# The opening of a transformer-stack kernel: order of the first transfers, and both token blocks worked on per k tile

## The reference

```python
f1 = swiglu(rms_norm(x, ffn1_pre_g), ffn1_w_gate, ffn1_w_up, ffn1_w_down)
# swiglu(x, g, u, d) = (silu(x @ g) * (x @ u)) @ d ; widths 1024 -> 2816 -> 1024
x = x + 0.5 * rms_norm(f1, ffn1_post_g)
# then a token mixer and two more FFNs; the mixer of block 2 (moba_attention)
# adds rel_bias_table_2[bucket(distance)] to its logits, with 32 buckets and 8 heads
```

## Time and profile before

| | us |
|---|---|
| median of 3 runs | 992.6 (992.57 to 992.99) |
| profiled execution: device time | 992.94 |
| profiled execution: span, first to last instruction | 991.1 |
| TensorE busy | 985.8 (99%) |
| VectorE busy | 711.4 (72%) |
| ScalarE busy | 486.5 (49%) |

### The profile page before, as it was taken

How to read it: one execution, slowest core, us unless ns; L and a number is a source line. 1 busy time by engine, 2 the same in 40 slices (tenths; PEclk the granted TensorE clock), 3 DMA queues, 4 the chain that set the end, 5 groups by cost and what they waited for, 6 DMA issues and landing times.

```text
span 991.1 us, 14543 instructions
## 1 busy us (share of the span) xinstructions
PE 985.8 (99%) x5302; PEld 835.6 (84%) x5302; DVE 711.4 (72%) x849; ACT 486.5 (49%) x621; POOL 213.2 (22%) x215
## 2 busy tenths in 40 slices
PE   8999999999999999999999999999999999999998
PEld 6888888888888888888888888888888888888887
DVE  5766767775788767676777998677876767666664
ACT  6534343664665533434545444465555445334342
POOL 3313232014100222222112600060000012223230
PEclk9999999999999999999999999999999999999999
DMA  9665656745325555565745625544536356555561
GB/s 311 227 211 171 208 173 199 268 128 192 127 87 170 203 179 204 176 203 178 240 156 177 204 95 196 190 145 148 170 118 222 129 187 233 170 179 201 179 206 44
DMA packets 121065, 178.53 MB, mean 180 GB/s; under 512 B 5808, under 2 KB 82160, under 8 KB 120896
## 3 DMA queue, kind: packets, MB, share of 16 engines
q1 hardware_dynamic: 120048, 174.86, 52.8%
q0 software_dynamic: 576, 1.39, 0.5%
q10 hardware_dynamic: 400, 1.73, 0.5%
HBM read 176.88 MB, written 2.64 MB: 181 GB/s over the span
## 4 chain that ended last, share of the span: by engine, by line
PE 99%; DMA 0%; ACT 0%; SPq 0%; DVE 0%; issue 0%
PE acc L662 11%; PE acc L666 10%; PE acc L665 10%; PE tp L861 10%; PE gu L861 10%; PE gu L866 5%; PE tp L866 5%; PE tp L662 4%; PE tp L666 4%; PE tp L665 4%; PE gu L662 3%; PE gu L666 3%; PE gu L665 3%; PE acc L1141 2%; PE acc L1144 1%; PE acc L1170 1%
## 5 line engine op out<-in xcount | busy, mean ns | idle before, releaser
L2001 DVE TENSOR_TENSOR wlo<-raw,whi 128x2048 fp32r<-128x2048 f32 x140 | 325.5, 2330 | 153.8 <-ACT whi L1361 152.2
L1361 ACT ACTIVATE whi<-raw 128x2048 fp32r<-128x2048 f32 x150 | 285.8, 1908 | 70.2 <-PE acc L666 22.9
L861 PE MATMUL tp<-act_in,whi 128*128 128x512 f32 x432 | 102.9, 390 | 0.0
L861 PE MATMUL gu<-act_in,whi 128*128 128x512 f32 x432 | 102.6, 390 | 0.0
L1898 POOL TENSOR_TENSOR tmp<-tmp 128x256 f32<-128x256 f32 x54 | 39.8, 737 | 276.2 <-DVE tmp L2122 276.2
L1900 POOL TENSOR_TENSOR sil<-sil,tmp 128x256 f32<-128x256 f32 x54 | 88.7, 1642 | 33.7 <-ACT sil L1432 33.7
L861 PEld LDWEIGHTS gu<-act_in,whi 128*128 128x128 f32 x432 | 80.9, 188 | 16.6
L662 PE MATMUL acc<-whi,hT_hi 128*128 128x512 f32 x240 | 94.0, 392 | 0.0
L665 PE MATMUL acc<-wlo,hT_hi 128*128 128x512 f32 x240 | 93.7, 390 | 0.0
L666 PE MATMUL acc<-whi,hT_lo 128*128 128x512 f32 x240 | 93.4, 389 | 0.0
L861 PEld LDWEIGHTS tp<-act_in,whi 128*128 128x128 f32 x432 | 79.8, 188 | 15.7
(11 more groups left out here) (379 smaller groups left out, 1845.0 us busy)
## 6 DMA issues: line engine op xcount, KB each, us to landing
raw<-in_w_in SPq DMA_DIRECT2D x96, 512.0 KB, 4.5
raw<-in_down SPq DMA_DIRECT2D x66, 512.0 KB, 4.1
raw<-in_gate SPq DMA_DIRECT2D x64, 512.0 KB, 4.3
raw<-in_up SPq DMA_DIRECT2D x64, 512.0 KB, 4.7
raw<-in_w_out SPq DMA_DIRECT2D x16, 512.0 KB, 4.7
raw<-in_w_branch_hg SPq DMA_DIRECT2D x8, 512.0 KB, 4.3
raw<-in_w_branch_attn SPq DMA_DIRECT2D x8, 512.0 KB, 4.7
post<-in_post_gains SPq DMA_DIRECT2D x3, 512.0 KB, 6.0
```

Source lines behind the costliest of these rows:

```text
L861: pe.matmul(banks[:, a, :], w_hi[:, i, a * P:(a + 1) * P], both, start=i == 0, stop=False)
L1361: act.activation(split_weights(k)[0], raw[:, k % RING, :], ACT.Copy).then_inc(hi_ready, 1)
L2001: dve.tensor_tensor(w_lo, raw[:, k % RING, :], w_hi.bitcast(F32), ALU.subtract).then_inc(lo_ready, 1)
```

## The change

- Head of `fixed` moves from ScalarE's queue to be SP's first transfer; x and piece 0 come in single k tiles (gate, up: 128 KB each) or quarters (x: 128 KB) in a new order. ScalarE issues up's k tiles 0 and 1 in its place. `hot` and `rel` become one array and one DMA.
- TensorE transposes k tiles 0 and 1 of each block as they come, multiplies each k tile of piece 0 for both token blocks before the next tile, and transposes tiles 2 and 3 of both blocks between the products of tiles 0 and 1. The warm-up between the transposes is 2 and 1 matmuls.
- The bias product moves behind the products of tiles 0 and 1, to another bank.
- ScalarE and VectorE follow that order; piece 1 is split by one k tile instead of two; `x_sums(0, 0)` comes after `fills(T_FFN1, 3)` instead of before piece 1's second part.

Cut to its core, with 8 columns of indent left out (the rest renames the input arrays):

```diff
...
 x_in = [sem(f"x_in{i}") for i in range(2 * TT)]
-part_in = [sem(f"part_in{i}") for i in range(4)]
+x_first = [sem(f"x_first{t}") for t in range(TT)]
+part_in = [sem(f"part_in{i}") for i in range(6)]
 tile_turned, tile_hi, tile_lo = sem("tile_turned"), sem("tile_hi"), sem("tile_lo")
 part_hi, part_lo, warm_ready, fixed_in = sem("part_hi"), sem("part_lo"), sem("warm_ready"), sem("fixed_in")
 head_in, bias_parts_in, tail_in = sem("head_in"), sem("bias_parts_in"), sem("tail_in")
...
 def first_bank(i, a):
-    return tp[:, a // 2, a % 2 * P:(a % 2 + 1) * P] if i else acc[:, a // 2, a % 2, 0:P]
+    banks = (tp[:, 0, :], acc[:, 1, 0, :], acc[:, 0, 1, :], tp[:, 1, :]) if i else \
+        (acc[:, 0, 0, :], acc[:, 0, 1, :], acc[:, 1, 1, :], acc[:, 0, 0, :])
+    return banks[a][:, 0:P]
 def first_place(i, a):
...
         for w, m in enumerate((wg_d[0], wu_d[0])):
             sp.dma_start(dst[:, 2 * a:2 * a + 2, w * FC:(w + 1) * FC],
                          m.rearrange("(k p) n -> p k n", p=P)[:, 4 * j + 2 * a:4 * j + 2 * a + 2, 0:FC])\
-              .then_inc(part_in[2 * j + a], 16)
+              .then_inc(part_in[4 + a], 16)
+    def x_quarter(t, q):
+        sp.dma_start(x[:, t, q * FC:(q + 1) * FC], x_d[t * P:(t + 1) * P, q * FC:(q + 1) * FC])\
+          .then_inc(x_in[2 * t] if q else x_first[t], 16)
+    def first_gate(a):
+        sp.dma_start(raw[:, 0, a * BLK:a * BLK + FC], wg_d[0][a * P:(a + 1) * P, 0:FC]).then_inc(part_in[a], 16)
+    def first_up(a):
+        sp.dma_start(raw[:, 0, a * BLK + FC:(a + 1) * BLK], wu_d[0][a * P:(a + 1) * P, 0:FC])\
+          .then_inc(part_in[a], 16)
     def first_pieces():
-        x_part(0, 0)
-        half_piece(0, 0)
-        x_part(1, 0)
-        half_piece(0, 1)
+        sp.dma_start(fixed[:, 0:G_END + P], fixed_d[:, 0:G_END + P]).then_inc(head_in, 16)
+        x_quarter(0, 0)
+        first_gate(0)
+        x_quarter(1, 0)
+        first_gate(1)
+        x_quarter(0, 1)
+        x_quarter(1, 1)
+        for a in (2, 3):
+            first_gate(a)
+            first_up(a)
         x_part(0, 1)
         half_piece(1, 0)
         x_part(1, 1)
...
         def turn(i):
             t, h = FILLS[u][i]
             pe.wait_ge(x_in[2 * t + h], 16)
-            if i >= 2:
-                fill(u, i, from_x)
-                return
-            for a in range(4):
-                mm = pe.transpose(first_bank(i, a), from_x(t, 4 * h + a), idn)
-                if a < 3 and (i == 0 or a == 1):
-                    mm.then_inc(tile_turned, 1)
-            mm.then_inc(turn_full, 1)
+            fill(u, i, from_x)
+        def turn_tile(i, a):
+            mm = pe.transpose(first_bank(i, a), from_x(FILLS[u][i][0], a), idn)
+            mm.then_inc(turn_full if a == 3 else tile_turned, 1)
         def product(j, t, a, rests=None):
             w_hi, w_lo = (w.rearrange("p (k n) -> p k n", k=4)[:, a, :] for w in split_weights(j))
...
         pe.wait_ge(warm_ready, 1)
         warm_up(7)
         pe.wait_ge(head_in, 16)
-        turn(0)
-        warm_up(3)
-        pe.wait_ge(bias_parts_in, 16 * 2)
-        pe.matmul(gu[0:8, 1, 0:S], rel[:, :], hot[:, :], start=True, stop=True).then_inc(row_product, 1)
-        for a in range(2):
-            pe.wait_ge(tile_lo, 1 + a)
-            pe.wait_ge(part_hi, 1 + a)
-            product(0, 0, a, rests=(part_lo, 1 + a))
-            if a == 0:
-                turn(1)
-        pe.wait_ge(row_copied, 1)
-        for a in range(2):
-            pe.wait_ge(tile_lo, 4 + a)
-            product(0, 1, a)
-        turn(2)
-        filled(u, 1)
+        for i in range(2):
+            pe.wait_ge(x_first[i], 16)
+            turn_tile(i, 0)
+            turn_tile(i, 1)
+            warm_up(2 - i)
+        pe.wait_ge(tile_lo, 1)
+        pe.wait_ge(part_hi, 1)
+        product(0, 0, 0, rests=(part_lo, 1))
+        pe.wait_ge(tile_lo, 2)
+        product(0, 1, 0)
+        pe.wait_ge(x_in[0], 16)
+        turn_tile(0, 2)
+        pe.wait_ge(x_in[2], 16)
+        pe.wait_ge(tile_lo, 3)
+        turn_tile(1, 2)
+        turn_tile(0, 3)
+        turn_tile(1, 3)
+        pe.wait_ge(part_hi, 2)
+        product(0, 0, 1, rests=(part_lo, 2))
+        pe.wait_ge(tile_lo, 4)
+        product(0, 1, 1)
+        pe.wait_ge(bias_parts_in, 16)
+        pe.matmul(acc[0:8, 1, 0, 0:S], rel, hot, start=True, stop=True).then_inc(row_product, 1)
+        pe.wait_ge(tile_lo, 5)
         pe.wait_ge(part_hi, 3)
         product(0, 0, 2, rests=(part_lo, 3))
+        turn(2)
+        pe.wait_ge(tile_lo, 6)
+        product(0, 1, 2)
+        filled(u, 1)
         pe.wait_ge(hi_ready, 1)
         product(0, 0, 3, rests=(lo_ready, 1))
         filled(u, 2)
-        product(0, 1, 2)
+        pe.wait_ge(row_copied, 1)
         turn(3)
         product(0, 1, 3).then_inc(piece_used, 1)
         filled(u, 3)
-        pe.wait_ge(part_hi, 4)
-        product(1, 0, 0, rests=(part_lo, 4))
-        product(1, 0, 1)
+        for a in range(3):
+            pe.wait_ge(part_hi, 4 + a)
+            product(1, 0, a, rests=(part_lo, 4 + a))
         pe.wait_ge(hi_ready, 2)
-        product(1, 0, 2, rests=(lo_ready, 2))
-        product(1, 0, 3).then_inc(gu_first, 1)
+        product(1, 0, 3, rests=(lo_ready, 2)).then_inc(gu_first, 1)
         filled(u, 4)
         for a in range(4):
             mm = product(1, 1, a)
...
         if m:
             act.wait_ge(x_half, bank_n(m - 1, t, 1))
         else:
+            act.wait_ge(x_first[t], 16)
             act.wait_ge(x_in[2 * t], 16)
             act.wait_ge(x_in[2 * t + 1], 16)
         if m or t:
...
     def first_hi(j, a, n):
         cut = slice(a * BLK, (a + n) * BLK)
-        act.wait_ge(part_in[2 * j + a // 2], 32)
+        act.wait_ge(part_in[4 + a // 2 if j else a], 32)
         act.activation(split_weights(j)[0][:, cut], raw[:, j, cut], ACT.Copy)\
            .then_inc(hi_ready if a + n == 4 else part_hi, 1)
-    def first_turned(i, *tiles):
-        for a in tiles:
-            if a == 3 or i and a == 2:
-                act.wait_ge(turn_full, i + 1)
-            else:
-                act.wait_ge(tile_turned, 4 if i else a + 1)
-            ins = act.activation(first_place(i, a)[0], first_bank(i, a), ACT.Copy, scale=first_gain(i, a))
-            if a == 3:
-                ins.then_inc(act_hi_ready, 1)
-            elif i == 0 or a == 1:
-                ins.then_inc(tile_hi, 1)
+    def first_turned(i, a):
+        if a == 3:
+            act.wait_ge(turn_full, i + 1)
+        else:
+            act.wait_ge(tile_turned, (5 if a == 2 else 2 * i + a) + (i if a == 2 else 1))
+        ins = act.activation(first_place(i, a)[0], first_bank(i, a), ACT.Copy, scale=first_gain(i, a))
+        ins.then_inc(act_hi_ready if a == 3 else tile_hi, 1)
     def row_from_bank():
         act.wait_ge(row_product, 1)
-        act.activation(proj[0:8, 0, 0:S], gu[0:8, 1, 0:S], ACT.Copy).then_inc(row_copied, 1)
+        act.activation(proj[0:8, 0, 0:S], acc[0:8, 1, 0, 0:S], ACT.Copy).then_inc(row_copied, 1)
     def first_setup():
...
         act.wait_ge(tail_in, 16 * 3)
         act.activation(fgw_split[:, :, 0, :], fgw[:, :, :], ACT.Copy).then_inc(act_setup, 1)
-    act.dma_start(fixed[:, 0:G_END + P], fixed_d[:, 0:G_END + P]).then_inc(head_in, 16)
-    for dst, src in ((hot[:, :], hot_d), (rel[:, :], rel_d)):
-        act.dma_start(dst, src).then_inc(bias_parts_in, 16)
+    for a in range(2):
+        act.dma_start(raw[:, 0, a * BLK + FC:(a + 1) * BLK], wu_d[0][a * P:(a + 1) * P, 0:FC]).then_inc(part_in[a], 16)
+    act.dma_start(bias_parts[:, :], bias_parts_d).then_inc(bias_parts_in, 16)
     act.wait_ge(pool_step, 1)
     load_table(0, ACT.Silu)
-    first_turned(0, 0, 1, 2)
+    first_turned(0, 0)
     first_hi(0, 0, 1)
-    first_turned(0, 3)
+    first_turned(1, 0)
+    first_turned(0, 1)
     first_hi(0, 1, 1)
+    first_turned(1, 1)
+    first_hi(0, 2, 1)
+    for a in (2, 3):
+        first_turned(0, a)
+        first_turned(1, a)
+    first_hi(0, 3, 1)
     row_from_bank()
-    first_turned(1, 0, 1, 2, 3)
-    first_hi(0, 2, 1)
-    first_hi(0, 3, 1)
-    first_hi(1, 0, 2)
+    first_hi(1, 0, 1)
+    first_hi(1, 1, 1)
     fills(T_FFN1, 2)
+    first_hi(1, 2, 1)
+    first_hi(1, 3, 1)
+    fills(T_FFN1, 3)
     x_sums(0, 0)
-    first_hi(1, 2, 2)
-    fills(T_FFN1, 3)
     hi(2)
     ffn(0, N_FFN1, N_WIN)
     act.wait_ge(row_out, 16)
...
         link(pool.memset(a[1][0:2, :, :], one))
     link(pool.memset(mhalf[:, :], -0.5))
-    pool.wait_ge(part_in[3], 32)
+    pool.wait_ge(part_in[5], 32)
     with nc.allow_non_contiguous_dma(reason="eight columns"):
         pool.dma_start(fgw[:, :, :], win_d.rearrange("(k p) n -> p k n", p=P)[:, :, FOX_GATE:FOX_GATE + 8])\
             .then_inc(tail_in, 16)
...
         if a + n == 4:
             dve.wait_ge(hi_ready, j + 1)
         else:
-            dve.wait_ge(part_hi, a + 1 if j == 0 else 4)
+            dve.wait_ge(part_hi, 3 * j + a + 1)
         w_hi, w_lo = split_weights(j)
```

(45 more changed lines are left out.)

## The result

| | median us | lowest to highest | runs |
|---|---|---|---|
| before | 992.69 | 992.28 to 993.22 | 22 |
| after | 994.23 | 993.50 to 994.99 | 22 |

The account below looks back on a forecast made before the run. TensorE bounds the kernel, busy 985.8 of 991.1 us, so only its 5.3 idle us can give time. First product -0.53, bias product +0.44, waits -0.66 sum to -0.75; likeliest gain 0.7, median 991.9 us, range 991.2 to 992.9.

Parts of the forecast that it names:

- Moved and free: Opening's transfers: smaller ones issue piece 2 at 8.9 instead of 7.1 us, but it still lands near 15.9, at no cost.
- the sum: Opening up to piece 2 on TensorE: -0.53 + 0.44 - 0.66 = -0.75 us, start at 19.82 instead of 20.57.
- Rival B: SP's queue in the opening: issues slow to 0.71 us, piece 2 lands 1.2 late, no gain, 992.6 us; 14%.
- chain behind piece 2: ScalarE reaches piece 2 at 16.2 us, VectorE's split of piece 3 ends at 25.8, TensorE wants it at 26.02.
- Rival C: TensorE before the first product: clock falls to 1.2 GHz for 3.2 us, +1.6 - 0.7, 993.5 us; 6%.
- First product: TensorE's first product of piece 0: starts at 6.70 instead of 7.23 us, 0.53 earlier (0.2 to 0.8).
- Rival D: Opening's transfers: each takes 4.3 us or more whatever its size, first product at 7.0, gain 0.4, 992.2; inside likeliest case's range.
- Bias product: TensorE, now between products instead of in the wait before the first: two passes 0.22 apart, 0.44 us later.
- Waits: TensorE between the opening's products: 0.3 us of waiting left instead of 0.96, so 0.66 earlier.
- The ceiling of 1.1: Later pieces: slacks at piece 3's split (1.20 less 0.2) and before `down` (1.16) limit any gain to some 1.1 us.

## Why the prediction was wrong

**Which step failed.** It is the sentence under "Moved and free": the bytes ahead of piece 2 are the same, so it lands near 15.9 still. It landed at 17.85. The bytes are the same, but not when they are handed over. At 6.4 us, eleven SP issues were out in both kernels: before 11 x 256 KB and ScalarE's 142, together 2,958 KB; after 109 + 10 x 128 and ScalarE's 289, together 1,678. SP's issues stand about 0.47 us apart whatever their size, so 128 KB each hand over at most some 280 GB/s where the stream could carry 377. The stream thinned out between 7.2 and 9.8, and piece 2 came 1.87 later. The runs bear this out from four sides: halved transfers alone cost 1.7 us, a late issue behind 256 KB transfers cost nothing, and fewer SP issues, by a second engine or by two 256 KB transfers, brought the rate back to 331 and 303 GB/s. But the full queue alone doesn't save the forecast. The order of work with the old transfers is still 1.1 us slower than before at the median, where the sum had a gain of 0.75. The second step that failed is the sum itself, whose terms follow below.

The prediction used as proof of a queue that is always full, while that fullness came from the 256 KB. It had the number in hand: 0.48 a transfer was its own term.

**Rival B** had the place and the price, and 14%: a late stream takes the gain from a delay of 1.2 on. The delay was 1.87. Its mechanism was off: it asked for issues that slow to 0.71, while they stayed near 0.47 but for one of 0.95, and a late issue behind a full queue moved piece 2 by 0.5 only and the time not at all. The prediction's chain behind piece 2 held: piece 2 on ScalarE 1.67 later than forecast (17.87 for 16.2) and the split of piece 3 at 25.8 + 1.67 = 27.47; measured 27.44.

**Rival C**, 6%, is seen in kernels near the changed one and not shown in it. Products at the lower level stand in three profiles: with up's tiles on ScalarE, where it came after 2.04 us without work, and with the early bias product and without the warm-ups, where the upper level had not been reached before. Removing three warm-ups from the kernel before makes some of its runs up to 2.4 us slower. But the changed kernel's own profile has the upper level, its 22 times form no two groups, and more warm-ups moved its median by 0.1 only. The rival can't be dismissed, and no run prices it there.

**The terms of the sum.** These are read from the two profiles and carry their scatter of some 0.3. First product: forecast 0.53 earlier, measured 0.32. Gate's tile 0 landed at about 6.1 instead of 5.7, so `whi` started at 6.13, and the same 0.77 as before leads to 6.90; x of block 1 (4.3 us to landing, issued at 2.13) held TensorE's list to the same moment. Rival D, a landing of 4.3 us or more whatever the size, had this part right. Bias product: forecast 0.44, measured 0.62 in the changed kernel and 0.63 put alone into the old one; the change between its small form and the products costs more than two passes 0.22 apart. Waits: forecast 0.3, and some 1.2 were left against 0.96 before; the one of 0.33 at 15.11 hangs on up of piece 1 landing late. So instead of 0.75 earlier piece 2 starts 0.32 earlier, 0.62 later and 0.27 later, together the 0.57 later that the timeline shows.

**What held.** The order for both blocks per k tile runs as simulated in the one profile in which its feeders were in time and the bias product early: piece 2 at 20.08, with waits of some 0.3. The ceiling of 1.1 wasn't put to the test: no version started piece 2 more than 0.49 earlier. The Trainium skill, DMA: Bandwidth & Descriptors, section Rules for kernel authors, had warned to coalesce; but it puts the overhead below 64 KB, and here 128 KB was too small, for the sake of the issue and not of the transfer. The same page, section Issuing engines are not separate DMA queues, calls the sequencer time that a second issuing engine saves usually small relative to the transfer. For one transfer the trace agrees, 0.43 us of issue against 4.3 to landing; but in the opening SP's issues follow one another, and two of them moved to ScalarE raised the stream from 222 to 331 GB/s.

**Still open.** Some 0.15 us of the loss lie outside the span: device time less span is 1.79 before and 1.94 after in the median, near 1.8 in every kernel with the old order of work and 1.85 to 2.02 in those with the new. No run here tells why; every kernel with the new order also has `hot` and `rel` merged into one array, and the two were not tried apart. The rest of the 1.54 us needs no further cause: 1.1 are the difference of the profiled spans, and 0.3 are there because the profiled execution before is slower than its median by 0.25 and the one after faster by 0.05. Nor is it shown how stream and order share the loss in an average execution, nor why the new order stays 0.6 above before with old transfers, early bias product and warm-ups.

## What to carry to other kernels

A DMA queue is fed in bytes per issue: divide the size of a transfer by the time from one issue to the next (here 128 KB by 0.47 us, some 280 GB/s) and compare it with what the stream carries (here 377); where the quotient is the smaller, splitting the transfers delays what lies behind them, however early the first piece lands. Two causes that delay different paths to the same wait do not add up, so removing one of them gives back less than it costs alone. Before work is thinned out ahead of the first matmuls, look at what keeps TensorE at its upper clock, and run often enough to see two groups of times. Where TensorE waits early, look first for an order of its own list that closes the wait, before touching the transfers: one moved line gave a likely 0.35 us here, where the whole reordering lost 1.5.

## What the runs showed of the hardware

- TensorE's rise to the upper level came at different times in executions of nearly the same opening: with the same seven warm-ups from 1.20 on, by 5.1 us in the kernel before, by about 6.6 and 7.5 in the ones with the late issue and with one line moved, and only at about 9.9 and 10.3 us in the profiled executions without the later warm-ups and with the early bias product.
- The granted clock in the windows read 1.00 over a stretch at the lower level in two kernels (early bias product, no warm-ups) while 512 columns stood 0.43 apart, and 0.59 in another (up's tiles on ScalarE). The Trainium skill, TensorE: Matmul & The Clock Gate, section Seeing it yourself, calls the recorded clock events unreliable; the trace agrees.
- Five transfers of 4 bytes a partition took 2.39 us to issue, 0.48 each; issues of 128 or 256 KB stood 0.47 apart.
- The bias product (8 rows by 256, two passes 0.22 us apart), put between large products, delayed the next instruction by 0.62 and 0.63 us.
